# Two attention layers with expert rows: layer 0's latents and the last layer as one program, the last layer's attention opened tile by tile behind the last expert sums

## The chip, the cores and the metric

The kernel runs on one core of one Trainium2 chip. The metric is the device time of one execution in microseconds (us), the median of the runs. Its engines are TensorE (PE; PEld is its weight load), VectorE (DVE), ScalarE (ACT), GpSimd (POOL) and SyncE (SP). SP, ACT and POOL issue DMAs on queues of their own (q1, q10, q0), which are served by the same 16 DMA engines.

## What is computed

A first block (two layers of mLSTM, MoBA and NSA mixers with a feed-forward of 4096) turns `x` [256, 1024] into the latents of a second block of two layers. Only the second block matters here. `c` stands for 256 context rows:

```
def second_block(x, c, ctx, ...):
    for i in range(2):
        h  = rms_norm(x, norm1_gain[i]) * (1 + sc1) + sh1;   hc = the same of xc with the context's rows
        q, k, v    = project_qkv(h, w_qkv[i], ...)    # 8 query heads, 2 key/value heads, 128 wide; rope for x only
        qc, kc, vc = project_qkv(hc, w_qkv[i], ...)
        o = latent_global_attention(...) if i == 0 else latent_window_attention(..., sink)   # 512 keys: 256 of x, 256 of xc
        x = x + g1 * (o @ w_o[i])
        if i == 0: xc = xc + cg1 * (context_attention(...) @ w_o[i])
        h2 = rms_norm(x, norm2_gain[i]) * (1 + sc2) + sh2
        x = x + g2 * peer_ffn(h2, ...)
        if i == 0: xc = xc + cg2 * peer_ffn(h2c, ...)
    return x

def peer_block(hb, w_q, sub_keys, u_tab, v_tab):     # per token: 8 heads x 16 experts out of 16384
    q = (hb @ w_q);  s1, s2 = its halves @ sub_keys;  top 16 of the sums of the top 16s -> expert, g = softmax
    act = gelu(u_tab[expert] . hb);  return sum((g * act) * v_tab[expert])
```

All is float32. So each of the 256 tokens needs 128 expert rows per layer, each a pair of u and v (2 x 1024 numbers, 8 KB).

## The kernel before

`build` (L2464) runs programs one after the other; each is a `Stage` (L101) with a block of instructions per engine, and `Stage.run` (L139) ends it with a barrier of all engines that also clears the semaphores. The order is: context attention; first block with the context's expert rows beside it (`Beside`, L1303); latents (`attention` with part "latents", then `experts` for layer 0, one program); last (`attention` with part "last", `experts` for layer 1, one program); and a last program that stores `x`.

PSUM is four pairs of banks. A stage lists its groups of matmuls in `order`; group number i gets pair i mod 4, one semaphore counts the groups computed, and one per pair counts how often it was emptied. So the list fixes PE's order.

`attention`, part "last" (`h_tiles` 0 to 3: tiles 0 and 1 are `x`, 2 and 3 the context). ACT issues the parameters' loads (L339 to L362): norm gain, context rows, mod rows. SP waits for the first mod rows (L300) and then loads three blocks of w_qkv into the three `ring` buffers, w_o after them (L309). DVE brings the context up to date (L558, L561), ACT squares all four tiles (L377), DVE norms all four (L551, L553), PE turns each (L168) and ACT copies them to `hT` (L383). PE then projects (L174) in the order K/V of tiles 0 and 1, K/V of 2 and 3, queries heads 0 to 3 of both tiles, heads 4 to 7. A block here means one tile by 512 columns, 16 matmul records: eight in all. DVE squares, norms and ropes keys and queries (`squared` L579, `finished` L593, POOL takes the power -0.5 at L762), PE turns them (`QT`), and a loop over 16 heads (tile, head) runs score, window add and maximum (L672, L674), exponential (L436), transposition and value product, with the first tile's output projection among the steps. Then `Early` (L1071) computes the query and scores of head 0, DVE routes it (`route_first` L1114), and POOL issues the first gathers while tile 1's output projection and second norm still run.

`experts` (L1025) has 16 turns (head f, tile g; tile 1 of head 7 last) of 16 rows, 256 in all, in batches of four. POOL gathers row n, one expert pair for each of 128 tokens, into slot n mod ns (`gather`, L1058). It waits until row n - ns is summed. DVE does the dot with `H` (L1148), and per batch the weights (L1151), ACT the tanh and four diagonals (L1218), PE the sums `acc` of v rows (L1267, L1273). ns is 14 for layer 0 and 15 for layer 1, of which 8 are free while the front still runs. SP loads w_q in 1 MB pieces into two halves of ring buffer 2. Queries, scores and routing of the turns ahead run between the batches. At the end DVE adds both tiles' sums to `x` (L1200, L1202), after all 256 rows.

## Time and profile before

| | us |
|---|---|
| median of 3 runs | 3256.99 |
| lowest, highest | 3243.01, 3263.39 |
| profiled execution, its own time | 3264.11 |
| span of its instructions | 3262.3 |
| PE busy in the span | 2631.4 (81%) |
| DVE busy | 1815.7 (56%) |
| POOL busy | 1266.9 (39%) |
| ACT busy | 479.6 (15%) |
| row gathers (q0), share of the 16 DMA engines | 62.2% |
| loads of SP's queue (q1), the same | 18.4% |

The profile is of one execution. A busy share is a mean over stages with different limits; so the slices and windows of the span are read first, and then the timeline of one stretch. In a timeline row the bracket at the end is the engine's idle time ahead of the instruction and what ended it.

### The profile page before, as it was taken

What the parts mean: (1) busy time and instruction counts of PE and PEld (TensorE: products, weight loads), DVE (VectorE), ACT (ScalarE), POOL (GpSimd) and SP (SyncE); (2) the same over time, 40 slices, a digit from 0 to 9 for tenths busy, and PEclk for the clock granted to TensorE, in tenths of its full rate; (3) what the DMA queues carried; (4) which work ended last, traced back from release to release, by engine and by line L of the source; (5) the groups of instructions that cost most, each with busy time, mean ns of one, the idle gap of its engine ahead of it and who ended that gap; (6) DMA issues with size and microseconds to landing.
All of it is one profiled execution on the core that took longest, in us unless ns stands there. A gap on an engine that the chain in (4) does not pass through costs nothing. (4 is left out here: it accounts for less than half of the span.)

```text
span 3262.3 us, 26724 instructions
## 1 busy us (share of the span) xinstructions
PE 2631.4 (81%) x8976; PEld 1410.5 (43%) x8976; DVE 1815.7 (56%) x4659; ACT 479.6 (15%) x1403; POOL 1266.9 (39%) x1072
## 2 busy tenths in 40 slices
PE   6786797999886699966778888888768788888876
PEld 2354555764433377421345343443334544334332
DVE  1438557687113256422148677777526677677774
ACT  0210221000111100000111111111112211111111
POOL 0000535452445367445534444454300254444442
PEclk9898886999997899977899999998978999999999
DMA  6656867797778679899859999999842499999996
GB/s 264 262 212 232 305 227 231 276 366 271 282 294 290 213 293 406 330 346 315 299 193 414 419 419 418 422 421 421 361 172 72 178 415 419 419 418 421 421 421 279
DMA packets 249212, 1046.83 MB, mean 321 GB/s; under 512 B 20550, under 2 KB 53430, under 8 KB 176884
## 3 DMA queue, kind: packets, MB, share of 16 engines
q0 software_dynamic: 147456, 805.37, 62.2%
q1 hardware_dynamic: 93456, 222.23, 18.4%
q10 hardware_dynamic: 8164, 17.53, 1.5%
q8 instruction: 72, 1.18, 0.1%
q14 instruction: 64, 0.52, 0.0%
HBM read 1041.28 MB, written 3.77 MB: 320 GB/s over the span
## 5 line engine op out<-in xcount | busy, mean ns | idle before, releaser
L1456 POOL DMA_INDIRECT sb_beside_slots<-in_peer_uv,sb_beside_chosen x256 | 357.4, 1396 | 394.5 <-DVE sb_beside_slots L1356 207.3
L1356 DVE SCALAR_TENSOR_TENSOR sb_beside_slots<-sb_beside_slots,sb_beside_H 128x1024 f32<-128x1024 f32 x256 | 304.2, 1220 | 120.4 <-DMA sb_beside_slots<-in_peer_uv,sb_beside_chosen 86.8
L1456 POOL DMA_INDIRECT sb_beside_slots<-in_peer_uv,sb_beside_small x256 | 249.8, 976 | 248.1 <-PE psum L1413 172.3
L174 PE MATMUL psum<-sb_f_arena,sb_f_ring 128*128 128x256 f32 (+1 forms) x1344 | 299.8, 386 | 9.3 <-issue 9.3
L174 PEld LDWEIGHTS psum<-sb_f_arena,sb_f_ring 128*128 128x128 f32 (+1 forms) x1344 | 253.4, 189 | 56.6 <-issue 13.9
L1413 PE MATMUL psum<-sb_beside_slots,sb_xc 128*32 128x512 f32 x1024 | 166.8, 783 | 120.3 <-DMA sb_beside_slots<-in_peer_uv,sb_beside_small 98.9
L174 PE MATMUL psum<-sb_f_ring,sb_f_arena 128*128 128x512 f32 (+2 forms) x448 | 191.9, 588 | 2.0 <-ACT sb_f_arena L1773 2.0
L1273 PE MATMUL psum<-sb_beside_slots,sb_latents_scores 128*128 128x512 f32 x304 | 151.2, 650 | 33.4 <-ACT sb_latents_scores L1228 33.3
L2403 PE MATMUL psum<-sb_f_ring,sb_f_arena 128*128 128x512 f32 x384 | 165.4, 592 | 0.0
L1273 PE MATMUL psum<-sb_latents_ring,sb_latents_scores 128*128 128x512 f32 x288 | 137.9, 630 | 26.7 <-ACT sb_latents_scores L1228 26.7
L1273 PE MATMUL psum<-sb_last_ring,sb_last_scores 128*128 128x512 f32 x272 | 129.9, 626 | 24.5 <-ACT sb_last_scores L1228 24.5
L1068 POOL DMA_INDIRECT sb_beside_slots<-in_peer_uv,sb_latents_scores x76 | 88.2, 1160 | 135.8 <-PE psum L1273 91.5
L174 PEld LDWEIGHTS psum<-sb_f_ring,sb_f_arena 128*128 128x128 f32 x448 | 85.8, 194 | 106.6 <-issue 103.8
L1068 POOL DMA_INDIRECT sb_latents_ring<-in_peer_uv,sb_latents_scores x72 | 91.0, 1264 | 92.4 <-PE psum L1273 85.5
L1413 PEld LDWEIGHTS psum<-sb_beside_slots,sb_xc 128*32 128x32 f32 x1024 | 35.1, 130 | 209.3 <-issue 185.9
L1148 DVE SCALAR_TENSOR_TENSOR sb_beside_slots<-sb_beside_slots,sb_latents_H 128x1024 f32<-128x1024 f32 x76 | 92.0, 1224 | 47.7 <-DMA sb_beside_slots<-in_peer_uv,sb_latents_scores 46.4
L1068 POOL DMA_INDIRECT sb_last_ring<-in_peer_uv,sb_last_scores x68 | 82.3, 1210 | 81.7 <-PE psum L1273 74.2
L2403 PEld LDWEIGHTS psum<-sb_f_ring,sb_f_arena 128*128 128x128 f32 x384 | 72.9, 190 | 91.4 <-issue 91.4
L1273 PEld LDWEIGHTS psum<-sb_beside_slots,sb_latents_scores 128*128 128x128 f32 x304 | 62.0, 208 | 115.6 <-issue 73.0
L1148 DVE SCALAR_TENSOR_TENSOR sb_latents_ring<-sb_latents_ring,sb_latents_H 128x1024 f32<-128x1024 f32 x72 | 87.0, 1224 | 42.5 <-DMA sb_latents_ring<-in_peer_uv,sb_latents_scores 42.5
L1148 DVE SCALAR_TENSOR_TENSOR sb_last_ring<-sb_last_ring,sb_last_H 128x1024 f32<-128x1024 f32 x68 | 82.1, 1223 | 34.6 <-DMA sb_last_ring<-in_peer_uv,sb_last_scores 34.6
L1273 PEld LDWEIGHTS psum<-sb_latents_ring,sb_latents_scores 128*128 128x128 f32 x288 | 56.8, 201 | 102.2 <-issue 66.3
(566 smaller groups left out, 4655.3 us busy)
## 6 DMA issues: line engine op xcount, KB each, us to landing
sb_f_ring<-in_w_ff SPq DMA_DIRECT2D x32, 2048.0 KB
sb_context_ring<-in_ada_w SPq DMA_DIRECT2D x23, 2048.0 KB, 13.3
sb_f_ring<-in_w_in SPq DMA_DIRECT2D x8, 2048.0 KB
sb_f_ring<-in_w_in SPq DMA_DIRECT2D x6, 1904.0 KB
sb_context_ring<-in_peer_w_q SPq DMA_DIRECT2D x8, 1024.0 KB, 10.1
sb_f_ring<-in_w_out SPq DMA_DIRECT2D x4, 2048.0 KB
sb_latents_ring<-in_peer_w_q SPq DMA_DIRECT2D x8, 1024.0 KB
sb_last_ring<-in_peer_w_q SPq DMA_DIRECT2D x8, 1024.0 KB, 25.4
```

Of the source, the lines that this page charges most:

```text
L174: last = e.matmul(out, a, b, start=(i == 0), stop=(i == len(terms) - 1))
L1068: e.indirect_dma_start(out=slots[n % ns], out_offset=None, in_=table, in_offset=bass.IndirectOffsetOnAxis(ap=rt["idx"][:, q % 4, k:k + 1], ...
L1148: e.scalar_tensor_tensor(out=u_of(n), in0=u_of(n), scalar=1.0, in1=H[:, turns[n // TOPK][0], :], op0=ALU.mult, op1=ALU.mult, accum_out=rt[ ...
L1273: done = e.matmul(st.pair(("acc", g))[:, half, :], diag[:, n % (4 * BATCH), :], v_of(n)[:, half * 512:(half + 1) * 512], start=(f == 0 and ...
L1356: e.scalar_tensor_tensor(out=row, in0=row, scalar=1.0, in1=self.H[:, t, :], op0=ALU.mult, op1=ALU.mult, accum_out=self.dots[t][:, s:s + 1] ...
L1413: done = e.matmul(self.sums[32 * j:32 * j + 32, half, :], self.columns[:, j, i % 16, :], rows[j][:, half * 512:(half + 1) * 512], start=(i ...
L1456: e.indirect_dma_start(out=self.slots[i % self.SLOTS], out_offset=None, in_=self.table, in_offset=bass.IndirectOffsetOnAxis(ap=at, axis=0) ...
L2403: done = e.matmul(acc[t][:, half, :], u_part[c][:, f * S + t * P:f * S + (t + 1) * P], w[:, f, half * 512:(half + 1) * 512], start=False, ...
```

## The change

The two last attention layers become one program. `last_attention` replaces part "last" of `attention`; it hands out an `Opening`, pieces that the first `experts` calls inside its last turn and behind it: `scalar_first` (square of tile 0), `vector_first_stats`, `vector_first` (norm of tile 0), `gpsimd_first`, `tensor_keys` (turning the sub keys, between the sums of batches 61 and 62), `tensor_first` (transposition and K/V projection of tile 0, behind the last sums), `scalar_first_turned` and `vector_context`. All loads of this attention are issued by SP, each behind a wait for the rows whose slot it overwrites.

The update of `x` is split by tile: tile 0, whose sums end with row 239, is added behind batch 60, tile 1 at the end. In the last layer each tile is stored once it is updated.

PE's order becomes: tile 0's transposition, K/V and first query block; tiles 2 and 3 with their K/V; tile 1 with its K/V; then query blocks one tile at a time. Tile 1's queries are normed and roped in the head loop's steps 1 to 3 and turned in steps 6 and 7.

Memory: layer 0 has 12 row slots instead of 14 (8 of them early, as before), since `gains` and `mod` are wanted earlier; layer 1 has 14 instead of 15, 9 of them early instead of 8. Its w_q pieces go through ring buffer 1.

The diff, cut to its core ("..." marks what is left out):

```diff
@@ def last_attention, new @@
+    order = ["subT", ("hT", 0), ("qkv", 2, 0), ("qkv", 0, 0), ("hT", 2), ("hT", 3), ("qkv", 2, 2), ("hT", 1), ("qkv", 2, 1),
+             ("qkv", 1, 0), ("QT", 0, 0), ("qkv", 0, 1), "KT", ("qkv", 1, 1), ("QT", 1, 0)]
+    tail = lambda g: [("oT", g), ("wo", g, 0), ("wo", g, 1), ("h2T", g)]
+    among = {6: ("QT", 0, 1), 7: ("QT", 1, 1), **dict(zip((9, 10, 12, 16), tail(0)))}
...
+    turns = [2, 3, 0] + [(2, 3, 0, 1)[i % 4] for i in range(len(order) - 3)]
+    st = Stage(nc, sems, psum, order, before.st, turns=turns)
...
+    def sync(e):
+        e.wait_ge(before.sc_copied, 2 * PH)
+        e.wait_ge(before.q_done, 2 * PH)
+        e.wait_ge(*before.landed(before.n_rows - 8))
+        e.dma_start(sub[:, 0:2, :], A["peer_sub_keys_2"][layer].rearrange("a k d -> k a d")).then_inc(sub_in, 16)
+        e.dma_start(gains[:, 0, :], A["norm1_gain_2"][layer:layer + 1, :].to_broadcast([P, D])).then_inc(gains_in[0], 16)
+        for j in (1, 0):
+            e.dma_start(mod[:, j, :], row_of(0, j)).then_inc(mods_in[0], 16)
+        e.dma_start(ring[2], chunk(wqkv, 2)).then_inc(w_in[2], 16)
+        e.wait_ge(before.added, before.n_rows - 8)
+        for j in (1, 0):
+            e.dma_start(modc[:, j, :], row_of(1, j)).then_inc(mods_in[1], 16)
+        for t in range(NT):
+            e.dma_start(work[:, t * D:(t + 1) * D], kept["xc"][:, t, :]).then_inc(xc_in, 16)
+        e.dma_start(work[:, 2 * D:3 * D], kept["mod0"][1:2, 5 * D:6 * D].to_broadcast([P, D])).then_inc(xc_in, 16)
+        e.wait_ge(before.added, before.n_rows - 6)
+        e.dma_start(ring[0], chunk(wqkv, 0)).then_inc(w_in[0], 16)
+        e.wait_ge(before.added, before.n_rows - 4)
+        e.dma_start(ring[1], chunk(wqkv, 1)).then_inc(w_in[1], 16)
+        for j, name in enumerate(("q_norm_gain_2", "k_norm_gain_2")):
+            e.dma_start(qkg[:, j, :], A[name][layer:layer + 1, :].to_broadcast([P, HD2])).then_inc(late_in, 16)
+        e.dma_start(sink[:, :], A["attn_sinks_2"][0:1, :].to_broadcast([P, H2])).then_inc(late_in, 16)
+        e.wait_ge(before.added, before.n_rows)
+        e.dma_start(sb["late"][:, :], A["late"]).then_inc(late_in, 16)
+        e.wait_ge(before.updated, NT)
+        e.dma_start(mod[:, 2, :], row_of(0, 2)).then_inc(gate_in, 16)
+        e.dma_start(gains[:, 1, :], A["norm2_gain_2"][layer:layer + 1, :].to_broadcast([P, D])).then_inc(gains_in[1], 16)
+        e.wait_ge(h_ready, 4)
+        for j in (1, 0):
+            e.dma_start(mod[:, j, :], row_of(0, 3 + j)).then_inc(mods_in[2], 16)
+        e.wait_ge(*st.computed(("qkv", 2, 1)))
+        e.dma_start(ring[wo_ring[0]], chunk(wo, 0)).then_inc(w_in[wo_ring[0]], 16)
+        e.wait_ge(*st.computed(("qkv", 0, 1)))
+        e.dma_start(ring[wo_ring[1]], chunk(wo, 1)).then_inc(w_in[wo_ring[1]], 16)
...
+    def scalar_first(e):
+        e.wait_ge(before.updated, 1)
+        squared_row(e, 0, H[:, 0, :])
+
+    def scalar_first_turned(e):
+        transposed(e, ("hT", 0))
+
+    def scalar(e, early):
+        e.wait_ge(before.added, before.n_rows)
+        kept_rows(e, 2, 0)
+        for g in (2, 3):
+            e.wait_ge(xc_ready, g - 1)
+            squared_row(e, g, work[:, 3 * D:4 * D] if g == 2 else flat(hTc, "p k n -> p (k n)")[:, 0:D])
+        e.wait_ge(before.updated, NT)
+        squared_row(e, 1, H[:, 1, :])
+        kept_rows(e, 0, 0)
+        transposed(e, ("hT", 2))
+        transposed(e, ("hT", 3))
+        transposed(e, ("hT", 1))
+        kept_rows(e, 2, 2)
+        kept_rows(e, 2, 1)
+        kept_rows(e, 1, 0)
...
+    def vector_first_stats(e):
+        deviation(e, rs1[:, 0:1], ss1[:, 0:1], 1)
+
+    def vector_first(e):
+        e.wait_ge(*st.computed("subT"))
+        e.tensor_copy(sub[:, 2:4, :].rearrange("p a n -> p (a n)"), st.pair("subT")[:, 0, 0:2 * P]).then_inc(*st.empties("subT"))
+        scaled(e, mod, 0, mods_in[0], 32)
+        normed(e, 0, rs1[:, 0:1], mod, 1)
+
+    def vector_context(e):
+        e.wait_ge(xc_in, 48)
+        for t in range(NT):
+            e.tensor_tensor(xs[2 + t], xs[2 + t], work[:, 2 * D:3 * D], ALU.mult).then_inc(*own.up())
+        e.wait_ge(*own.now)
+        for t in range(NT):
+            e.tensor_tensor(xs[2 + t], xs[2 + t], work[:, t * D:(t + 1) * D], ALU.add).then_inc(xc_ready, 1)
+        scaled(e, modc, 0, mods_in[1], 32)
+        deviation(e, rs1[:, 1:3], ss1[:, 1:3], 3)
+
+    def vector(e, early):
+        normed(e, 2, rs1[:, 1:2], modc, 2)
+        deviation(e, rs1[:, 3:4], ss1[:, 3:4], 4)
+        normed(e, 3, rs1[:, 2:3], modc, 2)
+        normed(e, 1, rs1[:, 3:4], mod, 3)
...
+        for turn, name in enumerate(((0, 0), "K", (1, 0))):
+            squared(name, work[:, 0:1024])
+            finished(name, 4 + turn, work[:, 1024:2048])
...
+            if i == 1:
+                squared((0, 1), later)
+            if i == 2:
+                finished((0, 1), 7, later)
+                squared((1, 1), later)
+            if i == 3:
+                finished((1, 1), 8, later)
+                scaled(e, mod, 1, mods_in[2], 32)
...
+    def gpsimd_first(e):
+        power(e, 1, rs1, 1)
+
+    def gpsimd(e, early):
+        for turn, (r, n) in enumerate(((rs1[:, 1:3], 2), (rs1[:, 3:4], 1), (rs[:, 0:4], 4), (rs[:, 32:40], 8), (rs[:, 8:12], 4), (rs[:, 4:8], 4), (rs[:, 12:16], 4), (rs2[:, 0:1], 1))):
+            power(e, turn + 2, r, n)
+        early.gather(e)
+        power(e, 10, rs2[:, 1:2], 1)
...
+    def tensor_keys(e):
+        e.wait_ge(sub_in, 16)
+        e.wait_ge(before.q_copied, 2 * PH)
+        ps = st.pair("subT")
+        flip(e, ps[:, 0, 0:P], sub[:, 0, :], ident)
+        flip(e, ps[:, 0, P:2 * P], sub[:, 1, :], ident).then_inc(st.mm, 1)
+
+    def tensor_first(e):
+        e.wait_ge(before.sc_copied, 2 * PH)
+        e.wait_ge(h_ready, 1)
+        transposes(e, ("hT", 0), hn(0))
+        e.wait_ge(before.updated, 1)
+        qkv(e, 2, 0)
+
+    def tensor(e, early):
+        qkv(e, 0, 0)
+        for g in (2, 3):
+            e.wait_ge(h_ready, g)
+            transposes(e, ("hT", g), hn(g))
+        e.wait_ge(before.updated, NT)
+        qkv(e, 2, 2)
+        e.wait_ge(h_ready, 4)
+        transposes(e, ("hT", 1), hn(1))
+        qkv(e, 2, 1)
+        qkv(e, 1, 0)
+
+        def queries_turned(c, g):
+            ps = opened(e, ("QT", c, g))
+            e.wait_ge(y_ready, {(0, 0): 1, (1, 0): 3, (0, 1): 4, (1, 1): 5}[c, g])
+            for j in range(4):
+                done = flip(e, ps[:, 0, j * P:(j + 1) * P], Y[:, g, (4 * c + j) * HD2:(4 * c + j + 1) * HD2], ident)
+            done.then_inc(st.mm, 1)
+
+        queries_turned(0, 0)
+        qkv(e, 0, 1)
+        ps = opened(e, "KT")
+        e.wait_ge(y_ready, 2)
+        for a in range(KV2):
+            for g in range(4):
+                done = flip(e, ps[:, a, g * P:(g + 1) * P], Y[:, g, (H2 + a) * HD2:(H2 + a + 1) * HD2], ident)
+        done.then_inc(st.mm, 1)
+        qkv(e, 1, 1)
+        queries_turned(1, 0)
+        e.wait_ge(*st.emptied("KT"))
+        for c in range(2):
+            e.wait_ge(*st.emptied(("QT", c, 0)))
...
@@ def experts @@
-    st = Stage(nc, sems, psum, [("acc", g) for g in range(NT)], front.st)
+    st = Stage(nc, sems, psum, [("acc", g) for g in range(NT)], front.st, signals=False)
-    wq_half = [sb["ring"][2][:, 2048 * j:2048 * (j + 1)].rearrange("p (k n) -> p k n", k=KT) for j in range(2)]
+    wq_half = [sb["wq_ring"][:, 2048 * j:2048 * (j + 1)].rearrange("p (k n) -> p k n", k=KT) for j in range(2)]
-    prod = u_of(0)
+    prod = sb["gains"][:, 1, :]
...
-        e.nop()
+        if out is not None:
+            tiles = out.rearrange("o (t p) d -> p (o t) d", p=P)
+            for g in range(NT):
+                e.wait_ge(updated, g + 1)
+                e.dma_start(tiles[:, g, :], xs[g]).then_inc(stored, 16)
+            e.wait_ge(stored, 16 * NT)
...
-        if n == ns - 2:
+        if n == n_early + 4:
...
+        if opening:
+            opening.gpsimd_first(e)
...
+        def update(g):
+            e.wait_ge(added, n_rows - (TOPK if g == 0 else 0))
+            e.wait_ge(*own.now)
+            if g:
+                e.wait_ge(updated, g)
+            e.tensor_tensor(prod.rearrange("p (b n) -> p b n", b=2), st.pair(("acc", g))[:, :, :], mod[:, 2, :].rearrange("p (b n) -> p b n", b=2), ALU.mult).then_inc(*own.up())
+            e.wait_ge(*own.now)
+            e.tensor_tensor(xs[g], xs[g], prod, ALU.add).then_inc(updated, 1)
...
+                if b == n_rows // BATCH - 4:
+                    update(0)
+                if opening and b == n_rows // BATCH - 3:
+                    opening.vector_first_stats(e)
+                if opening and b == n_rows // BATCH - 2:
+                    opening.vector_first(e)
             if ahead(q):
                 keep_scores(ahead(q))
-        for g in range(NT):
-            if g == 0:
-                e.wait_ge(added, n_rows)
-            e.wait_ge(*own.now)
-            e.tensor_tensor(prod.rearrange("p (b n) -> p b n", b=2), st.pair(("acc", g))[:, :, :], mod[:, 2, :].rearrange("p (b n) -> p b n", b=2), ALU.mult).then_inc(*own.up())
-            e.wait_ge(*own.now)
-            e.tensor_tensor(xs[g], xs[g], prod, ALU.add).then_inc(*own.up())
-
-    def scalar(e):
+        if opening:
+            opening.vector_context(e)
+        update(1)
...
+            if opening and q == len(turns) - 1:
+                opening.scalar_first(e)
...
             if ahead(q):
                 scores(ahead(q))
+            if opening and q == len(turns) - 1:
+                opening.tensor_keys(e)
             sums(4 * q + 2)
             sums(4 * q + 3)
-
-    st.run(sync, scalar, vector, gpsimd, tensor, beside and beside.sems[0])
+        if opening:
+            opening.tensor_first(e)
...
@@ def layer_memory, def last_memory (new) @@
-    slots = [*spare]
-    if last:
-        at = 3584 + ROUTE_COLS
-        slots += [mod[:, 3:5, :].rearrange("p k n -> p (k n)"), pair(H, 1)]
-        slots += [big[:, at + 2048 * j:at + 2048 * (j + 1)] for j in range(2)]
-    slots += [work[:, 0:2048], work[:, 2048:4096], aux[:, 0:2048]]
-    sb["n_early"] = len(slots)
-    slots += [ring[:, j // 2, 2048 * (j % 2):2048 * (j % 2 + 1)] for j in range(4)]
-    slots += [flat(sb["hT2"][:, :, :], "p k n -> p (k n)")[:, 2048:4096]] if last else []
-    slots += [pair(gains, 0), pair(mod, 0)]
-    sb["slots"] = slots
+    halves = lambda j: [ring[:, j, 0:2048], ring[:, j, 2048:4096]]
+    flat_pair = lambda a, j: flat(a[:, 2 * j:2 * j + 2, :], "p k n -> p (k n)")
+    early = [flat_pair(spare, j) for j in range(3)] + [aux[:, 0:2048], flat_pair(spare, 3), flat(beside_H[:, :, :], "p t n -> p (t n)"), work[:, 0:2048], work[:, 2048:4096]]
+    sb["slots"], sb["n_early"], sb["wq_ring"] = early + halves(0) + halves(1), len(early), sb["ring"][2]
+    return sb
+
+
+def last_memory(sb, spare, beside_H, xc):
+
+
+    sb = dict(sb)
+    early = [flat(xc[:, :, :], "p t n -> p (t n)")] + sb["slots"][0:sb["n_early"]]
+    sb["Y"] = flat(spare[:, 0:6, :], "p k n -> p (k n)").rearrange("p (g n) -> p g n", g=4)
+    sb["hTc"] = flat(spare[:, 6:8, :], "p k n -> p (k n)").rearrange("p (k n) -> p k n", k=KT)
+    sb["modc"] = beside_H
+    sb["QT2"] = sb["big"][:, 0:5120].rearrange("p (h n) -> p h n", h=10)
+    halves = lambda r: [r[:, 0:2048], r[:, 2048:4096]]
+    sb["slots"] = early + halves(sb["ring"][2]) + halves(sb["ring"][0]) + [flat(sb["mod"][:, 0:2, :], "p k n -> p (k n)")]
+    sb["n_early"], sb["wq_ring"] = len(early), sb["ring"][1]
...
@@ def build @@
+                former = experts(nc, sems, psum, sb, A, C, xs, 0, front, beside)
+                front, opening = last_attention(nc, sems, psum, sb_last, A, C, xs, kept, former)
+                latter = experts(nc, sems, psum, sb_last, A, C, xs, 1, front, out=out)
...
+                def sync(e):
+                    former.sync(e)
+                    latter.sync(e)
...
+                latter.st.run(sync, scalar, vector, gpsimd, tensor, beside.sems[0])
```

## Rows read from the trace of the kernel before

**Rows 1.** The page, part 2: GB/s moved in 40 slices of 81.56 us.

```profile
GB/s 264 262 212 232 305 227 231 276 366 271 282 294 290 213 293 406 330 346 315 299 193 414 419 419 418 422 421 421 361 172 72 178 415 419 419 418 421 421 421 279
```

**Rows 2.** Windows from:to, width, busy us (instructions) per engine, TensorE clock, DMA share, GB/s.

```profile
2200.00:2300.00 100.00, 83.16 (x168) 34.31 (x167) 71.26 (x199) 17.51 (x64) 47.82 (x42) 0.90 1.01 421
...
2360.00:2380.00 20.00, 12.03 (x24) 4.69 (x22) 7.86 (x11) 1.69 (x6) 0.00 (x0) 0.84 0.01 4
...
2420.00:2440.00 20.00, 20.00 (x48) 8.79 (x47) 0.00 (x0) 1.02 (x1) 0.00 (x0) 1.00 0.00 1
...
2500.00:2520.00 20.00, 17.93 (x108) 12.48 (x107) 16.34 (x46) 9.25 (x26) 0.00 (x0) 1.00 0.00 1
```

**Rows 3.** Timeline (start us, us, engine, line, operation, idle before and releaser), POOL.

```profile
2571.99 1.01 POOL L1068 DMA_INDIRECT sb_xc<-in_peer_uv,sb_last_scores  x1 [22.57 <-DVE sb_last_scores L1139]
```

**Rows 4.** Timeline, DVE: the dots of row 248 and of row 255.

```profile
2345.96 1.22 DVE L1148 SCALAR_TENSOR_TENSOR sb_latents_ring<-sb_latents_ring,sb_latents_H 128x1024 f32<-128x1024 f32 x1 [0.32 <-DMA sb_latents_ring<-in_peer_uv,sb_latents_scores]
...
2363.29 1.23 DVE L1148 SCALAR_TENSOR_TENSOR sb_beside_slots<-sb_beside_slots,sb_latents_H 128x1024 f32<-128x1024 f32 x1 [1.23 <-DMA sb_beside_slots<-in_peer_uv,sb_latents_scores]
```

**Rows 5.** Timeline, PE; the line without an engine's form is of the chain of waits.

```profile
2365.95 8.83 PE L1273 MATMUL psum<-sb_beside_slots,sb_latents_scores 128*128 128x512 f32 x16 [2.76 <-ACT sb_latents_scores L1228]
...
2413.98 57.11 PE L174 MATMUL psum<-sb_last_ring,sb_last_hT 128*128 128x512 f32 x128 [1.43 <-ACT sb_last_hT L383]
...
2413.98 43.39 PE psum L174 x96
...
2487.60 3.75 PE L880 MATMUL psum<-sb_last_scores 128*128 128x512 f32 x4 [0.88 <-ACT sb_last_scores L417]
...
2556.72 3.48 PE L174 MATMUL psum<-sb_last_hT,sb_last_ring 128*128 128x128 f32 x29 [0.27 <-issue]
```

**Rows 6.** Timeline, ACT's first load of layer 1 and the scale row.

```profile
2381.09 0.30 ACTq L339 DMA_DIRECT2D sb_last_crow<-in_c  x1
...
2396.94 2.36 DVE L538 SCALAR_TENSOR_TENSOR sb_last_mod<-sb_last_mod,sb_last_gains 128x1024 f32<-128x1024 f32 x2 [0.84 <-DMA sb_last_mod<-kept_mod]
```

**Rows 7.** Timeline, one mod row and its taker; tile ring of layer 1, loads, issue to landing.

```profile
2578.01 0.33 ACTq L468 DMA_DIRECT2D sb_last_mod<-kept_mod  x1
...
2586.53 1.22 DVE L1148 SCALAR_TENSOR_TENSOR sb_xc<-sb_xc,sb_last_H 128x1024 f32<-128x1024 f32 x1 [1.57 <-DMA sb_last_mod<-kept_mod]
...
DMA to landing us min/median/max: 8.3/25.1/32.8
```

**Rows 8.** Timeline, DVE: a rope instruction, and the first operation of three heads.

```profile
2480.55 0.42 DVE L612 TENSOR_TENSOR sb_last_work<-sb_last_scores,sb_last_aux 128x256 f32<-128x256 f32 x1
...
2489.68 0.69 DVE L672 TENSOR_TENSOR sb_last_work<-psum,sb_last_aux 128x512 f32<-128x512 f32 x1 [3.85 <-PE psum L880]
...
2500.67 0.68 DVE L672 TENSOR_TENSOR sb_last_work<-psum,sb_last_aux 128x512 f32<-128x512 f32 x1
...
2505.95 0.69 DVE L672 TENSOR_TENSOR sb_last_work<-psum,sb_last_aux 128x512 f32<-128x512 f32 x1 [0.18 <-PE psum L880]
```

**Rows 9.** Timeline, POOL and DVE: first gather of layer 0, dot of row 7.

```profile
1693.12 0.99 POOL L1068 DMA_INDIRECT sb_beside_slots<-in_peer_uv,sb_latents_scores  x1 [24.08 <-DVE sb_latents_scores L1139]
...
1719.69 1.23 DVE L1148 SCALAR_TENSOR_TENSOR sb_latents_aux<-sb_latents_aux,sb_latents_H 128x1024 f32<-128x1024 f32 x1 [1.26 <-DMA sb_latents_aux<-in_peer_uv,sb_latents_scores]
```

**Rows 10.** Timeline, POOL: gather of row 119; DVE: dot of row 117.

```profile
1998.99 1.04 POOL L1068 DMA_INDIRECT sb_latents_aux<-in_peer_uv,sb_latents_scores  x1 [1.94 <-PE psum L1273]
...
2011.63 1.23 DVE L1148 SCALAR_TENSOR_TENSOR sb_latents_work<-sb_latents_work,sb_latents_H 128x1024 f32<-128x1024 f32 x1 [0.38 <-DMA sb_latents_work<-in_peer_uv,sb_latents_scores]
```

**Rows 11.** Timeline, POOL and DVE: gather and dot of row 30.

```profile
1773.52 1.32 POOL L1068 DMA_INDIRECT sb_beside_slots<-in_peer_uv,sb_latents_scores  x1 [3.19 <-PE psum L1273]
...
1784.08 1.23 DVE L1148 SCALAR_TENSOR_TENSOR sb_beside_slots<-sb_beside_slots,sb_latents_H 128x1024 f32<-128x1024 f32 x1 [0.72 <-DMA sb_beside_slots<-in_peer_uv,sb_latents_scores]
```

**Rows 12.** Timeline, the end: last dot, last update instruction, store.

```profile
3241.50 1.23 DVE L1148 SCALAR_TENSOR_TENSOR sb_xc<-sb_xc,sb_last_H 128x1024 f32<-128x1024 f32 x1 [1.25 <-DMA sb_xc<-in_peer_uv,sb_last_scores]
...
3255.16 1.22 DVE L1202 TENSOR_TENSOR sb_x<-sb_x,sb_xc 128x1024 f32<-128x1024 f32 x1
...
3257.52 0.38 SPq L2510 DMA_DIRECT2D out<-sb_x  x1
```

423 lines of the change are left out of this document (332 added, 91 removed).

## Prediction

> **What bounds the kernel now.** Read the slices of the page first. The row of GB/s is the one to follow: in slices 22 to 28 it stands near 420, falls to 172, 72 and 178 for three slices of 81.6 us, and comes back to 415 to 422 until near the end [rows 1]. The two plateaus are the expert stages of the two attention layers. The windows say the same at closer range: 421 GB/s at a DMA share of 1.01 with PE busy 83 of 100 us in the first plateau, then 4 and 1 GB/s between the two [rows 2]. In the plateaus the DMA engines are the bound: each row gather moves 128 x 8 KB = 1.05 MB, and the last eight dots start 2.48 us apart (17.33 us for seven steps), each after a wait for its gather [rows 4].
>
> POOL issues the first gather of layer 1 at 2571.99 [rows 3]; the last dot of layer 0 starts at 2363.29 [rows 4]. For 208.7 us no gather runs. The last stage then needs 3241.50 - 2571.99 = 669.5 us from its first gather to its last dot, the one before needed 2363.29 - 1693.12 = 670.2 [rows 3, 4, 9, 12]. So what pulls the gather at 2571.99 forward pulls the end forward by as much, unless a plateau becomes slower. I follow the chain through this gap.
>
> **The gap in pieces.** Row 248, the first of the last eight, starts its dot at 2345.96 [rows 4]; I call this A. The last sums run on PE from 2365.95 to 2374.78, A+28.8; I call their end T [rows 5]. Then come the update of x, the barrier, loads issued from 2381.09 on, a scale row that waits for one of them until 2396.94 [rows 6], four norms and transposes, eight blocks of projection from 2413.98 on (57.1 us), norms and turning of the queries, and the first scores at 2487.60, T+112.8 [rows 5]. The heads last to 2556.72, 69.1 us. The early query, the routing of one head and the first gather take 15.3 us more.
>
> **What is taken out and added up to the heads.** The barrier goes, and the loads' wait in series, and the norm of all four tiles ahead of any projection. Norm, transposition and K/V projection of tile 0 go around the last expert sums. Before T this costs:
> - The update of tile 0 (two DVE instructions of 1.22 us [rows 12], 2.5) moves ahead of the dots of batch 61. DVE is free for 1.23 us in front of a dot [rows 4], so two rows take it up: nothing.
> - At A, SP issues the sub keys (0.13 MB), a gain and two mod rows (1.6 MB) and 2 MB of w_qkv. DVE waits for the first four in `vector_first`. Behind this wait stand the four dots of batch 63, their weights, ACT's diagonals and PE's last sums; nothing fills it. How long is it? Alone, loads pass quickly: the shortest weight load (1 MB) lands after 8.3 us. But seven gathers are in flight, and beside gathers the longest took 32.8. One mod row of the same size, issued at 2578.01 into running gathers, lets DVE go at 2586.53, 8.5 us [rows 7]. I take 8.5 for the first such row, 4 for each of the two behind it in the same queue, 5.5 for the small one: A+22. Bounds: A+11 (hardly held up; then the last gather's landing sets the dots) and A+31 (8.5 for each).
> - From A+22: scale row 1.2, norm 2.5, four dots without a wait 4.6, weights and diagonals 1.4 (2364.52 to 2365.95), sums 8.8 [rows 4 to 6] gives the new end of the sums, T' = A+40.5. T was A+28.8: 11.7 us later (bounds 4 and 21).
>
> The Trainium skill (DMA: Bandwidth & Descriptors, Queues, rings and completion order) says that each DMA engine goes round its queues packet by packet. If one load and one row gather took turns, a mod row would cost 1.25 + 2.5 = 3.75 us and three 11.3. By this estimate the sum would be some 5 us better; the 8.5 us row bears on it and is slower.
>
> After T' the PE order is: transposes, K/V and first queries of tile 0, transposes and K/V of tiles 2 and 3, the same of tile 1, then three query blocks with the turning of queries and keys between them. PE sets this stretch:
> - Eight blocks, as many as now. Six with their slow start take 43.39, the last two 57.11 - 43.39 = 13.7, so 6.87 each [rows 5]: 55.0.
> - Flips: four transposes of 1.1, turning 0.5, 1.0 and 0.6 (eight flips take 1.04 to 1.1): 6.5.
> - Waits, from laying the engines side by side: ACT's copy of hT 1.6. DVE's norms of tiles 2 and 3, 2.0 and 1.5; they start only when the update of tile 1 is through at T'+15.8, since DVE first waits for ACT's squares of the context, which stand behind K/V of tile 0 (T'+12.9). Copies of 1.4, 1.4 and 1.0. Sum 8.9.
>
> Together 70.4 against 112.8: 42.4 less. The barrier itself is small in it (four updates end at 2379.8, ACT issues at 2381.09). K's DVE work and the POOL powers lie beside projections; if that cover went, K's 10 us would stand in PE's way. The rest of q1's traffic, 8 MB with two more w_qkv blocks and the context rows, is through near A+46, ahead of each use; the late constants, issued at T', are wanted at T'+27.
>
> **The heads.** DVE now norms and turns the second tile's queries inside head steps 1 to 3. For each of two blocks: a square and a reduce of 0.69 (512 columns), 0.17, two multiplications of 0.69, six rope instructions 0.34 apart [rows 8], 5.0. With the scale row, 1.2, that now runs ahead of the loop: 11.3. Two heads take 5.28 us (2500.67 to 2505.95 [rows 8]) with DVE busy 16.3 and PE 17.9 of 20 us [rows 2]: little room. But before the first head's scores DVE waits 3.85 us [rows 8], and the first three heads run slower than the rest; I take 3.4 of this as gone. 69.1 + 11.3 - 3.4 = 77.0, 7.9 more (bounds 0 and 12). The tail as now, 15.3.
>
> First gather: 11.7 - 42.4 + 7.9 = 22.8 us earlier.
>
> **The slots.** The first plateau gets 12 row slots instead of 14, the second 14 instead of 15. The second change costs nothing: with 14 and 15 slots the plateaus took 670.2 and 669.5. For 12, ask what a gather needs when nothing is queued: issued at 1693.12; the eighth dot waits until 1719.69; less seven rows of 2.48, 9.2 us [rows 9]. With two slots fewer a gather is issued when today the one two places on is. In steady running the tightest place leaves 2011.63 - 1998.99 = 12.6 us, over 9.2 [rows 10]. In the start-up a row issued at 1773.52 has its dot at 1784.08 with 14 slots [rows 11]: no queue is left, and two slots fewer lose 1 to 4 us in each of one or two places. I take 4 (0 to 10).
>
> The same page (Anatomy of one DMA) gives 2 us plus bytes over 436 GB/s, here 4.4 us. By that the slots would cost nothing; no row here shows so short a gather.
>
> **The end.** Of four update instructions two run ahead, the store is half as large and follows without a barrier (3256.38 to 3257.52 now [rows 12]): 2.5 + 1.1 + 0.6 = 4.2 (3 to 6).
>
> **Sum.** -22.8 + 4 - 4.2 = -23.0. The profiled execution took 3264.1 (span 3262.3), so 3241; against the median of 3257.0, 7 lower, 3234.
>
> **Rivals.**
> - *Short waits:* the loads land by A+11 and the head steps hide DVE's extra work. For it, DVE's 3.85 us ahead of the heads; against it, 16.3 of 20 us busy after. -23 - 7.7 - 7.9 = -39: 3218.
> - *The loads hold DVE longer,* 8.5 us each. For it, the 32.8. T' is 9 later: 3243.
> - *Slower: 12 slots starve the first plateau.* A slot's round trip is now 14 x 2.48 = 34.7 us. If that were latency and not queueing, 12 slots would give a row every 2.89 us: 256 rows, 105 more, 3335. It takes the whole gain (27 us without the 4) from a round trip of 31.0 on (0.105 us a row), and is 1% slower from 32.6. Against: the rows above met 2.48 with 10.6 and 12.6 us in hand [rows 10, 11].
> - *No change in effect:* T' 21 later, heads 12 longer, slots 10: 21 - 42.4 + 12 + 10 - 4.2 = -4: 3253.
>
> **How the numbers follow.** The forecast case (3226 to 3241) has 0.57, short waits 0.18, longer loads 0.13, no effect 0.07, starved 0.05. The range holds all but the starved case and the outer ends of two others: 3214 to 3253. About 1% (32.6 us) is what a measurement can tell, so 3224.4 and 3289.6 are the bounds. Faster needs most of the short waits, or slots that cost nothing beside part of them: 0.20. Slower is the starved case: 0.05. The rest, 0.75, is within 1%.
>
> **What would show it.** Right: the first gather of layer 1 comes some 19 us sooner; before the last four dots DVE waits about 10 us for mod rows, and then they run back to back; PE idles under 10 us between T' and the heads; the head loop is some 8 us longer; both plateaus at 418 to 421 GB/s. Wrong: a first plateau under 415 GB/s, a wait for mod rows under 4 or over 20 us, PE gaps ahead of the heads, or a head loop of 69 us.

## The result, and the profile of the kernel after

The changed kernel takes 3239.3 us (median of 20 runs, 3233.8 to 3246.1), the kernel before 3258.6 (20 runs, 3243.0 to 3266.3). The ratio is 0.9944, interval [0.9936, 0.9952]: 19.3 us less, 0.6%. The forecast was 23 us less. The profiled execution of after has a span of 3237.4 us, that of before 3262.3.

The page of after, its slices of DMA share and GB/s (40 equal slices of 80.9 us):

```profile
DMA  6656866797778679989859999999952599999996
GB/s 266 263 190 243 294 239 217 276 385 278 279 267 314 240 273 406 360 325 319 305 180 391 419 419 419 420 421 417 421 192 78 204 407 418 419 418 421 421 421 288
```

Beside [rows 1], the two plateaus stand at the same height, the hole between them is filled a little (192, 78, 204 for 172, 72, 178), and the first plateau starts lower: the 100 us that begin 10 us after its first gather have 395 GB/s, in before 414. From 20 us after the first gather on, 620 us of the first plateau have 416 GB/s (before: 419).

The two gathers at the hole's rims, on POOL, timeline of after (start, duration, engine, line, operation, in brackets the idle time before it and who ended it):

```profile
2339.47 0.95 POOL L1501 DMA_INDIRECT sb_second_aux<-in_peer_uv,sb_second_scores  x1 [0.30 <-issue]
2547.59 1.01 POOL L1501 DMA_INDIRECT sb_xc<-in_peer_uv,sb_second_scores  x1 [22.05 <-DVE sb_second_scores L1583]
```

The first gather of layer 1 is issued at 2547.59, against 2571.99 in [rows 3]: 24.4 us sooner. Of these, 7.0 are no work of the change: the first gather of layer 0 came at 1686.17 in this execution and at 1693.12 in that of before [rows 9], and everything up to there is unchanged. 17.4 us are left.

The place where DVE waits for the mod rows, timeline of DVE in after (the short accumulator reads left out):

```profile
2342.10 1.23 DVE L1592 SCALAR_TENSOR_TENSOR sb_second_ring<-sb_second_ring,sb_second_H 128x1024 f32<-128x1024 f32 x1 [0.24 <-DMA sb_second_ring<-in_peer_uv,sb_second_scores]
...
2362.58 1.23 DVE L1082 SCALAR_TENSOR_TENSOR sb_second_mod<-sb_second_mod,sb_second_gains 128x1024 f32<-128x1024 f32 x1 [10.02 <-DMA sb_second_mod<-kept_mod]
2363.92 1.28 DVE L1091 SCALAR_TENSOR_TENSOR sb_second_H<-sb_x,sb_second_small,sb_second_mod 128x1024 f32<-128x1024 f32 x1
2365.24 1.23 DVE L1093 TENSOR_TENSOR sb_second_H<-sb_second_H,sb_second_mod 128x1024 f32<-128x1024 f32 x1
2366.38 1.22 DVE L1592 SCALAR_TENSOR_TENSOR sb_beside_slots<-sb_beside_slots,sb_second_H 128x1024 f32<-128x1024 f32 x1
2367.52 1.22 DVE L1592 SCALAR_TENSOR_TENSOR sb_beside_slots<-sb_beside_slots,sb_second_H 128x1024 f32<-128x1024 f32 x1
```

A is 2342.10, the dot of row 248. The mod rows let DVE go at A+20.5 after 10.02 us of idle time; scale row, norm, and then the four dots 1.15 us apart, as forecast.

PE from the last sums to the heads, timeline of PE in after:

```profile
2372.48 7.40 PE L1723 MATMUL psum<-sb_beside_slots,sb_second_scores 128*128 128x512 f32 x12 [12.80 <-ACT sb_second_scores L1674]
2379.72 1.88 PE L1723 MATMUL psum<-sb_second_aux,sb_second_scores 128*128 128x512 f32 x4
2381.43 1.04 PE L171 MATMUL psum<-sb_consts,sb_second_H 128*128 128x128 f32 x8
2383.68 13.97 PE L177 MATMUL psum<-sb_second_ring,sb_second_hT 128*128 128x512 f32 x32 [1.21 <-ACT sb_second_hT L1001]
2398.68 1.09 PE L171 MATMUL psum<-sb_consts,sb_xc 128*128 128x128 f32 x8 [1.03 <-DVE sb_xc L1093]
2401.20 1.09 PE L171 MATMUL psum<-sb_consts,sb_xc 128*128 128x128 f32 x8 [1.43 <-DVE sb_xc L1093]
2403.50 15.67 PE L177 MATMUL psum<-sb_second_ring,sb_beside_slots 128*128 128x512 f32 x32 [1.21 <-ACT sb_beside_slots L1001]
...
2451.60 1.96 PE L1342 MATMUL psum<-sb_second_scores 128*128 128x512 f32 x4 [0.94 <-ACT sb_second_scores L1035]
2455.33 0.63 PE L171 MATMUL psum<-sb_consts,sb_second_work 128*128 128x128 f32 x4 [1.78 <-ACT sb_second_work L1056]
...
2468.31 0.76 PE L171 MATMUL psum<-sb_consts,sb_second_work 128*128 128x128 f32 x4 [4.92 <-ACT sb_second_work L1056]
...
2475.66 1.09 PE L171 MATMUL psum<-sb_consts,sb_second_work 128*128 128x128 f32 x4 [3.31 <-ACT sb_second_work L1056]
```

The last sums end at 2381.6 (A+39.5) and the first scores start at 2451.60: 70.0 us, where [rows 5] had 112.8. In the head loop PE stands still for 4.92 and 3.31 us; in both places it waits for ACT's exponentials, and these for DVE's maxima, which stand behind tile 1's query work in DVE's order. DVE itself stood idle ahead of the loop, before its first instruction:

```profile
2452.73 0.69 DVE L1196 TENSOR_TENSOR sb_second_work<-psum,sb_second_aux 128x512 f32<-128x512 f32 x1 [7.21 <-PE psum L1342]
```

The end, timeline of after:

```profile
3219.11 1.23 DVE L1592 SCALAR_TENSOR_TENSOR sb_beside_slots<-sb_beside_slots,sb_second_H 128x1024 f32<-128x1024 f32 x1 [1.24 <-DMA sb_beside_slots<-in_peer_uv,sb_second_scores]
...
3230.64 1.22 DVE L1554 TENSOR_TENSOR sb_second_gains<-psum,sb_second_mod 128x1024 f32<-128x1024 f32 x1 [9.36 <-PE psum L1723]
3231.90 1.22 DVE L1556 TENSOR_TENSOR sb_x<-sb_x,sb_second_gains 128x1024 f32<-128x1024 f32 x1
3233.15 0.36 SPq L1488 DMA_DIRECT2D out<-sb_x  x1
```

Two update instructions instead of four, and the store right behind them; the last dot is 18.3 us before the end, 20.8 in before [rows 12].

### The profile page after: what moved, and what is told of

The parts are those of the page before. It is cut to its first block, busy times and chain, and to the rows that moved or that the text cites. A ratio compares the mean times of both kernels' runs of the same rounds, so it can differ in the third digit from the quotient of the medians.

```text
span 3237.4 us, 26712 instructions
## 1 busy us (share of the span) xinstructions
PE 2627.7 (81%) x8974; PEld 1406.6 (43%) x8974; DVE 1817.8 (56%) x4670; ACT 479.7 (15%) x1406; POOL 1257.0 (39%) x1076
## 3 DMA queue, kind: packets, MB, share of 16 engines
HBM read 1041.27 MB, written 3.77 MB: 323 GB/s over the span
## 4 chain that ended last, share of the span: by engine, by line
DMA 23%; PE 21%; DVE 7%; POOL 3%; issue 2%; ACT 1%; SPq 0%; DVEq 0%; another core or an unknown queue 0%; ACTq 0%; POOLq 0%
PE psum L1723 11%; PE psum L177 7%; DMA sb_beside_slots<-in_peer_uv,sb_second_scores 5%; DMA sb_second_ring<-in_peer_uv,sb_second_scores 5%; DMA sb_second_work<-in_peer_uv,sb_second_scores 3%; DMA sb_second_aux<-in_peer_uv,sb_second_scores 3%; DMA sb_beside_slots<-in_peer_uv,sb_beside_small 2%; PE psum L1867 2%; DMA sb_second_ring<-in_peer_w_q 2%; POOL sb_beside_slots L1910 1%; DMA sb_second_mod<-in_peer_uv,sb_second_scores 1%; DMA sb_second_mod<-kept_mod 1%; POOL sb_beside_slots L1501 1%; DVE sb_second_scores L1430 1%; DVE sb_second_scores L1433 1%
## 5 line engine op out<-in xcount | busy, mean ns | idle before, releaser
L1723 PE MATMUL psum<-sb_beside_slots,sb_second_scores 128*128 128x512 f32 x648 | 334.7, 662 | 97.1 <-ACT sb_second_scores L1674 95.6
L1723 PE MATMUL psum<-sb_second_ring,sb_second_scores 128*128 128x512 f32 x624 | 302.1, 636 | 60.5 <-ACT sb_second_scores L1674 60.5
L1501 POOL DMA_INDIRECT sb_beside_slots<-in_peer_uv,sb_second_scores x162 | 199.1, 1229 | 282.8 <-PE psum L1723 222.0
L1501 POOL DMA_INDIRECT sb_second_ring<-in_peer_uv,sb_second_scores x156 | 196.7, 1261 | 200.2 <-PE psum L1723 184.4
L1723 PEld LDWEIGHTS psum<-sb_beside_slots,sb_second_scores 128*128 128x128 f32 x648 | 134.0, 212 | 275.6 <-issue 155.7
L1592 DVE SCALAR_TENSOR_TENSOR sb_second_ring<-sb_second_ring,sb_second_H 128x1024 f32<-128x1024 f32 x156 | 188.5, 1223 | 91.2 <-DMA sb_second_ring<-in_peer_uv,sb_second_scores 90.9
L1592 DVE SCALAR_TENSOR_TENSOR sb_beside_slots<-sb_beside_slots,sb_second_H 128x1024 f32<-128x1024 f32 x162 | 195.9, 1222 | 76.0 <-DMA sb_beside_slots<-in_peer_uv,sb_second_scores 75.0
L1674 ACT ACTIVATE sb_second_scores<-sb_consts,sb_second_scores 128x128 f32<-128x128 f32 x512 | 163.8, 391 | 38.5 <-DVE sb_second_scores L1604 34.9
L1723 PE MATMUL psum<-sb_second_work,sb_second_scores 128*128 128x512 f32 x312 | 148.3, 615 | 13.0 <-ACT sb_second_scores L1674 13.0
L177 PE MATMUL psum<-sb_second_ring,sb_second_hT 128*128 128x512 f32 x320 | 141.3, 598 | 3.7 <-ACT sb_second_hT L1001 1.9
```

What stands on the lines that cost most here:

```text
L177: last = e.matmul(out, a, b, start=(i == 0), stop=(i == len(terms) - 1))
L1501: e.indirect_dma_start(out=slots[n % ns], out_offset=None, in_=table, in_offset=bass.IndirectOffsetOnAxis(ap=rt["idx"][:, q % 4, k:k + 1], ...
L1592: e.scalar_tensor_tensor(out=u_of(n), in0=u_of(n), scalar=1.0, in1=H[:, turns[n // TOPK][0], :], op0=ALU.mult, op1=ALU.mult, accum_out=rt[ ...
L1674: e.activation(diag[:, (b % 4) * BATCH + r, :], C("ident"), ACT.Copy, scale=w[:, r:r + 1]).then_inc(diag_ready, 1)
L1723: done = e.matmul(st.pair(("acc", g))[:, half, :], diag[:, n % (4 * BATCH), :], v_of(n)[:, half * 512:(half + 1) * 512], start=(f == 0 and ...
```

## The experiments

Each experiment was profiled, so it can be read by its stages as well as by its time. The stages matter here: over the 14 profiled executions the first gather of layer 0 came anywhere from 1685.5 to 1697.2 us, though all of them do the same work up to there. The table gives, for each profile: from the first gather of layer 0 to A; from A to the start of the last dot; from A to the end of the last sums (T); from T to the first scores; from there to the first gather of layer 1; the sum, first gather to first gather; from there to the last dot; from it to the end. All were worked out from starts and durations in the timelines of POOL, DVE and PE. The last column is the median time. Eight kernels are the same up to A (after, norm_late, loads_late, loads_series, kv_after_norms, heads_moved, no_tile1_work, combo); their first stage takes 654.8 to 657.0 us, so some 2 us in one row of this column are scatter. The medians come from four comparisons in which before itself stood at 3258.6, 3259.7, 3261.2 and 3261.8 us; kernels of different comparisons are set side by side by their ratios to before.

| kernel | gather to A | last dot | T | to scores | to gather | gather to gather | to last dot | to end | median |
|---|---|---|---|---|---|---|---|---|---|
| before | 652.8 | A+17.3 | A+28.8 | 112.8 | 84.4 | 878.9 | 669.5 | 20.8 | 3258.6 |
| before_again | 653.0 | A+17.4 | A+27.2 | 111.0 | 82.8 | 874.0 | 669.5 | 22.5 | 3258.9 (one run) |
| slots_only | 655.2 | A+17.3 | A+27.2 | 109.8 | 82.8 | 874.9 | 670.5 | 22.5 | 3264.6 |
| after | 655.9 | A+27.7 | A+39.5 | 70.0 | 96.0 | 861.4 | 671.5 | 18.3 | 3239.3 |
| rows_early | 660.4 | A+21.5 | A+33.7 | 70.8 | 95.8 | 860.7 | 670.7 | 16.5 | 3241.2 |
| all_early | 665.4 | A+19.0 | A+31.3 | 70.8 | 95.8 | 863.3 | 670.8 | 16.6 | 3242.3 |
| norm_late | 657.0 | A+22.0 | A+34.6 | 71.0 | 95.9 | 858.5 | 671.5 | 18.3 | 3239.9 |
| loads_late | 654.8 | A+17.8 | A+30.5 | 71.2 | 95.9 | 852.4 | 670.8 | 16.6 | 3231.3 |
| loads_series | 655.8 | A+17.8 | A+29.3 | 85.3 | 95.7 | 866.0 | 671.0 | 16.6 | 3243.9 |
| kv_after_norms | 655.3 | A+27.7 | A+39.9 | 80.0 | 96.2 | 871.4 | 670.6 | 16.6 | 3249.4 |
| heads_moved | 655.7 | A+27.7 | A+40.2 | 70.9 | 88.2 | 854.9 | 671.8 | 16.5 | 3236.5 |
| no_tile1_work | 655.3 | A+27.8 | A+40.0 | 70.8 | 84.2 | 850.3 | 670.7 | 18.1 | 3234.3 |
| combo | 655.9 | A+17.8 | A+27.6 | 73.9 | 88.2 | 845.6 | 670.6 | 18.2 | 3226.5 |
| combo_rows | 659.8 | A+17.3 | A+27.2 | 69.9 | 88.2 | 845.0 | 671.8 | 16.5 | 3228.7 |

The theory on trial is the sum of the prediction: loads that hold DVE ahead of the last sums, a shorter way from there to the heads, DVE's extra work in the heads, a few us for the slots. The rivals are that the wait has another nature, that the heads hide the work, and that the slots cost nothing or much.

**The wait for the mod rows: three ways to be rid of it.** The first, rows_early, issues the same rows sooner:

```
-        e.wait_ge(*before.landed(before.n_rows - 8))
+        e.wait_ge(*before.landed(before.n_rows - 24))
         e.dma_start(sub[:, 0:2, :], ...)
         ...                                    # gain, two mod rows
+        e.wait_ge(*before.landed(before.n_rows - 8))
         e.dma_start(ring[2], chunk(wqkv, 2))
```

> Kernel after, but the sub keys, the gain and the two mod rows of tile 0 are issued 16 rows (about 40 us) sooner; w_qkv stays where it was. Theory (the loads' wait stands on the path of the last sums): DVE's idle 10.0 us before the scale row goes, while 1.7 MB pass among the gathers instead, at 419 GB/s 4.1 us that row 248 comes later. Net 6 us less than after: about 3233 us. Rival A (bandwidth is not tight enough to matter): the full 10 us, 3229. Rival B (the end of the last sums does not set what follows, because the w_qkv block or the squares do): the wait goes but K/V of tile 0 starts no sooner, 3239 or a few us more.

Measured: 3241.2 us, ratio to before 0.9945 [0.9929, 0.996], where after has 0.9944. My 3233 was wrong, and rival B's number (3239 or a few more) came true, but not its cause: K/V of tile 0 does start sooner, at A+35.8 for A+41.6. The price was right: first gather to A is 4.5 us longer, for 1.7 MB. But the last dot comes only 6.2 us sooner, not 10: with the rows there, two of the last four dots wait for their gathers by 1.17 and 2.02 us. What was gained at the last sums (5.8) was mostly paid in the plateau (4.5).

The second, all_early, is the first hunk without the second, so w_qkv goes early too:

> As rows_early, but the first w_qkv block (2.1 MB) goes with the rows 16 rows sooner. Theory (in the plateau every byte costs its time at 419 GB/s): row 248 comes 5.0 us later than in rows_early, and nothing waits less for it, so 5 us more than rows_early, 3238. Rival A (room is left beside the gathers): the same as rows_early. Rival B (the w_qkv block held K/V of tile 0 back): less than rows_early.

Measured: 3242.3 us, 0.9955 [0.9939, 0.9971]. First gather to A grows by another 5.0 us for another 2.1 MB, exactly the bandwidth's price. But the last sums come 2.4 us sooner (A+31.3 for A+33.7), since this block no longer passes beside the last gathers; I had expected no such return. Gather to gather is 2.6 over rows_early, not 5; the two medians can't be told apart.

The third, norm_late, leaves the loads and moves the waiting instruction:

```
-                if opening and b == n_rows // BATCH - 2:
-                    opening.vector_first(e)
         ...
         if opening:
+            opening.vector_first(e)
             opening.vector_context(e)
```

> Kernel after, but the scale row and the norm of tile 0 stand behind the dots and weights of the last batch instead of ahead of them. Theory (the placement itself made the last sums wait for the mod rows): the last dots wait only for their gathers, the last sums end at A+29 instead of A+39.5 (A: start of the dot of row 248), DVE has the scale row at about A+21.7 and the norm at A+24.2, still ahead of the end of the sums, so the transposes of tile 0 start up to 10 us sooner: 3230 us, range 3228 to 3234. Rival (the norm is then late for PE, by scale row, norm and the copies, some 5 us or more in series after the sums, and the loads are late as well): 3237 to 3243.

Measured: 3239.9 us, 0.9935 [0.9922, 0.9949]; I had expected 3230. The rival's range, 3237 to 3243, holds it, and half of its cause is there: the loads are late, but the norm is not, since the transposes follow the last sums without a pause. By its time it can't be told from after; by stages it is 2.9 us better, gather to gather (4.1 from A on), and the reason why it is not 9 stands in its last four dots, timeline of DVE in norm_late:

```profile
2361.43 1.23 DVE L1592 SCALAR_TENSOR_TENSOR sb_beside_slots<-sb_beside_slots,sb_second_H 128x1024 f32<-128x1024 f32 x1 [1.05 <-DMA sb_beside_slots<-in_peer_uv,sb_second_scores]
...
2365.20 1.22 DVE L1592 SCALAR_TENSOR_TENSOR sb_beside_slots<-sb_beside_slots,sb_second_H 128x1024 f32<-128x1024 f32 x1 [2.53 <-DMA sb_beside_slots<-in_peer_uv,sb_second_scores]
...
2368.97 1.23 DVE L1592 SCALAR_TENSOR_TENSOR sb_beside_slots<-sb_beside_slots,sb_second_H 128x1024 f32<-128x1024 f32 x1 [2.53 <-DMA sb_beside_slots<-in_peer_uv,sb_second_scores]
...
2372.45 1.23 DVE L1592 SCALAR_TENSOR_TENSOR sb_second_aux<-sb_second_aux,sb_second_H 128x1024 f32<-128x1024 f32 x1 [2.25 <-DMA sb_second_aux<-in_peer_uv,sb_second_scores]
```

Nothing of DVE's own stands between them, and yet they are 3.77, 3.77 and 3.48 us apart instead of 2.48. The loads slow the gathers themselves. So the 10.02 us in after were not only a wait of one instruction behind its loads: behind it stood gathers that were late as well, hidden by it. The Trainium skill (DMA: Bandwidth & Descriptors, Queues, rings and completion order) says that a DMA engine goes round its queues packet by packet, so a queue of loads takes turns with the queue of gathers; the spacing, 3.77 us for 2.48, agrees in kind.

**The loads behind the last gather.** If loads and gathers share, the loads should start when the gathers are through. On top of norm_late:

```
         e.dma_start(sub[:, 0:2, :], ...)
+        e.wait_ge(*before.landed(before.n_rows - 1))
         e.dma_start(gains[:, 0, :], ...)
```

> As norm_late, and the gain, the mod rows and the first w_qkv block are issued only once the last row gather has landed (the sub keys stay where they were). In norm_late the last four dots were 3.5 to 3.8 us apart instead of 2.48 and the last sums ended at A+34.6. Theory (the wait is not one of order but of bytes: loads and the last gathers share the DMA engines): with nothing beside them the last dots are 2.48 apart again, last dot A+17.3, last sums A+28.8; gain and rows then land alone, some 6 to 9 us after A+17, norm at A+27 to A+30, w_qkv before A+34. First scores about A+100 to A+103 against 105.5 in norm_late and 109.5 in after: 3233 to 3237 us. Rival (a fixed cost of each load, not the sharing, spaced the dots): last dot at A+22 again and the loads later still, so 3 us or more slower than norm_late, 3243.

Measured: 3231.3 us, 0.9915 [0.99, 0.9929], a little under the 3233 to 3237 expected; the first scores come at A+101.7, as expected. Gather to gather is 9.0 us under after; 1.1 of these lie ahead of A, where the two kernels are the same, so 7.9 are the placement's, and 3.8 of them come on top of norm_late. The last dots, timeline of DVE in loads_late, are 2.46 to 2.48 us apart again, and then DVE waits for the mod rows with no dot behind it:

```profile
2356.62 1.23 DVE L1593 SCALAR_TENSOR_TENSOR sb_beside_slots<-sb_beside_slots,sb_second_H 128x1024 f32<-128x1024 f32 x1 [1.24 <-DMA sb_beside_slots<-in_peer_uv,sb_second_scores]
...
2359.08 1.23 DVE L1593 SCALAR_TENSOR_TENSOR sb_second_aux<-sb_second_aux,sb_second_H 128x1024 f32<-128x1024 f32 x1 [1.23 <-DMA sb_second_aux<-in_peer_uv,sb_second_scores]
...
2367.61 1.23 DVE L1083 SCALAR_TENSOR_TENSOR sb_second_mod<-sb_second_mod,sb_second_gains 128x1024 f32<-128x1024 f32 x1 [6.02 <-DMA sb_second_mod<-kept_mod]
```

The rows, issued from 2359.07 on, are there at 2367.61, 8.5 us later, and the norm ends at 2371.5, just as the last sums end at 2371.8. That settles the nature of the wait: the same bytes, started some 17 us later, cost 3.8 us less than in norm_late, which differs in nothing else, because they no longer stand in the way of the gathers that the last sums need. The rival with a fixed cost of each load (last dot at A+22 again) is out.

**How much the overlapped loads and the early K/V are worth.** Two undoings. In loads_series the wait of loads_late is on the last expert sum instead (`e.wait_ge(before.added, before.n_rows)`), so that the loads come in series behind the sums, without a barrier:

> As loads_late, but the gain, rows and w_qkv blocks are issued only when the last expert sum is added, so that they come in series as in before; no barrier, tile order kept. Theory (loads in series cost their whole landing, the barrier itself little): issue at A+29, rows land 9 us later, norm and transposes 5 more; K/V of tile 0 starts at A+44 instead of A+33, first scores 10 to 12 us later than in loads_late (A+101.7), 3242 us. Rival (the barrier was what cost, so that loads in series are nearly as good): within 4 us of loads_late.

Measured: 3243.9 us, 0.9937 [0.9919, 0.9955]. First scores at A+114.6 against A+101.7, 12.9 us later, a little over the 10 to 12 expected. (The ratios of the times, 0.9937 and 0.9915, are 7 us apart, and with four and five runs their intervals overlap; the size is read from the stages.) DVE waits 17.39 us for the mod rows and PE 12.44 us for the norm. And this kernel, with its loads as late as before's but no barrier and tile order, still takes 85.3 us from the last sums to the first scores, where before takes 110 to 113. In kv_after_norms PE waits for all four norms ahead of K/V of tile 0, and ACT squares the context first:

```
         e.wait_ge(before.updated, 1)
+        e.wait_ge(h_ready, 4)
         qkv(e, 2, 0)
```

> Kernel after, but the K/V projection of tile 0 waits until all four norms are through (ACT squares the context ahead of keeping it), as in before; program, loads and slots as in after. Theory (42.4 us between the last sums and the first scores come partly from tile 0 being projected while the others are normed): the four norms end about 13 us after the last sums instead of K/V starting at 2.3 us after them, two to four us of waits further on go: first scores 7 to 9 us later than in after, at T+77 to T+79 (after: T+70.0), 3247 us. Rival (the projections wait later anyway for loads or copies, so the early start gains nothing): T+70 to T+72, 3240.

Measured: 3249.4 us, 0.996 [0.9947, 0.9974]; 80.0 us to the scores instead of 70.0, one more than the top of my range. The row, timeline of PE in kv_after_norms:

```profile
2401.55 16.48 PE L177 MATMUL psum<-sb_second_ring,sb_second_hT 128*128 128x512 f32 x32 [13.28 <-DVE sb_second_H L1093]
```

In after PE has 14 us of projections to do while ACT squares and DVE norms the context and tile 1; here it stood idle for 13.28. And 2.5 of the 10.0 us are the clock: these 32 matmuls took 16.48 us at a granted clock of 0.85, and 13.97 at 1.00 in after. So by stages more than half of the change's gain is this one placement. By the ratios of the times it is less, 5 us, and the intervals overlap a little.

**The heads.** First, how much of the loop's growth is DVE's work on tile 1: no_tile1_work leaves out its queries' norm, gain and rope, with two instructions of four columns in place of each block, and puts the second norm's scale row in step 9:

```
             if i == 1:
-                squared((0, 1), later)
+                skipped((0, 1), 7)
             ...
```

> Kernel after without the norm, gain and rope of tile 1's queries (left out: their squares, reduces, scales and rotations, two instructions of four columns stand in for each block), and the scale row in step 9. Theory (DVE's extra work of 11.3 us lies on the path whole): first scores to first gather falls from 96.0 to 84.4, the value of before; 3228 us. Rival (part of the loop's growth is PE's, from its clock or from the turning of tile 1's queries): 88 or more stays.

Measured: 84.2 us from the first scores to the first gather; before has 84.4, and 82.8 in two other profiles. The growth, 11.8 us, is DVE's 11.3 and next to nothing else; no part of it was hidden. (Against 82.8 the growth is 13.2, and 1.4 of it have no shown cause.) Its time is 3234.3 us, 0.9912 [0.9897, 0.9927]: not the 3228 expected, but by the ratios 10 us under after.

heads_moved keeps the work and places it better:

```
         for turn, name in enumerate(((0, 0), "K", (1, 0))):
             ...
+        squared((0, 1), H[:, 1, :])
+        finished((0, 1), 7, H[:, 1, :])
         ...
-            if i == 1:
-                squared((0, 1), later)
             if i == 2:
-                finished((0, 1), 7, later)
                 squared((1, 1), later)
-            if i == 3:
+            if i == 4:
                 finished((1, 1), 8, later)
+            if i == 9:
                 scaled(e, mod, 1, mods_in[2], 32)
```

> Kernel after, but the first query block of tile 1 is squared and normed ahead of the head loop, where DVE waited 7.2 us, the second is squared in step 2 and finished in step 4, and the scale row goes from step 3 to step 9. Theory (DVE's 11.3 us of extra work in steps 1 to 3 lie on the path whole): 5.0 us go into the wait ahead of the loop and 6.3 are spread over steps that have about 0.4 us free each, so first scores to first gather of layer 1 falls from 96.0 to 89 to 91; 3233 to 3235 us. Rival A (the loop is held by PE's half-clock stretches): 96 stays, 3239. Rival B (DVE is full in all steps, so that a spread saves nothing and only the 5.0 of the wait count): 91.

Measured: 88.2 us in the stage, 7.8 less, a little better than either version expected; 3236.5 us, 0.9925 [0.9912, 0.9939], by the ratios 6 us under after (expected 3233 to 3235). Timeline of DVE in heads_moved, the last instruction ahead of the loop and the first one in it:

```profile
2452.30 0.42 DVE L1164 TENSOR_TENSOR sb_beside_slots<-sb_second_H 128x256 f32<-128x256 f32 x1
2453.38 0.69 DVE L1198 TENSOR_TENSOR sb_second_work<-psum,sb_second_aux 128x512 f32<-128x512 f32 x1 [0.66 <-PE psum L1342]
```

The idle time ahead of the first head was 7.21 us in after and is 0.66 here. The first block fits into it whole; of the remaining 6.3 us, moved to steps with a little room, some 2.8 vanish too. The rival that PE's clock holds the loop is out.

**The slots.** The kernel before with 12 slots in the first expert stage and 14 in the second, otherwise as it was:

```
-        if n == ns - 2:
+        if n == n_early + 4:
         ...
-    slots += [flat(sb["hT2"][...])[:, 2048:4096]] if last else []
-    slots += [pair(gains, 0), pair(mod, 0)]
+    slots += [pair(gains, 0)] if last else []
+    slots += [pair(mod, 0)] if last else []
```

> Kernel before with 12 row slots in the first expert stage and 14 in the last, nothing else changed. Theory (the start-up of the first plateau loses by the two slots, the rest does not): first gather to dot of row 248 3.1 us longer than in before (as it is in after), last plateau within 1 us: 3 us more than before. Rival A (the slots cost nothing and the 3.1 us of after have another cause): same as before. Rival B (the last plateau loses too, 2 us, as in after): 5 us more.

Measured: 3264.6 us, 1.0015 [1.0006, 1.0024], 4.9 us over the 3259.7 of before in the same comparison. By stages 2.4 (or 2.2, against before_again) are in the first plateau and 1.0 in the second. The loss is in the first 100 us, as forecast: the dot of row 24 comes 79.9 us after the first gather (before: 79.7), that of row 32 at 103.2 (99.4), that of row 60 at 175.1 (172.6), and from there on 2.4 us stay. Window view of 1700 to 1800 us in slots_only (busy time of each engine with its instructions, granted clock, DMA share, GB/s), where before has 413 and after 396 GB/s:

```profile
1700.00:1800.00 100.00, 76.47 (x238) 44.67 (x239) 73.90 (x214) 18.20 (x63) 45.02 (x38) 0.91 0.99 397
```

The interval reaches from 2 to 8 us, so the theory's 3 and rival B's 5 are not told apart by the times; "no cost" is out, and starvation is out by far. For the first plateau the eight kernels that are the same up to A bear it out: 654.8 to 657.0 us, where before has 652.8 and 653.0. By the sum of the Trainium skill for a DMA (DMA: Bandwidth & Descriptors, Anatomy of one DMA: 4.4 us for a gather by its figures, an estimate), the slots would have cost nothing; these stages show that they cost 2 to 4 us.

**Both improvements together.** combo is loads_late and heads_moved in one, with the scale row in step 10:

> loads_late and heads_moved together, the scale row for the second norm one step later still (step 10, where DVE waited 6.7 us). Theory (both lie in series on the one path): first gather to first gather of the two stages 861.4 - 9.0 - 7.8 - 1.2 = 843 us, 3222 us, 1.1% under before. Rival (what the first gives the second loses, in the clock or in waits for copies): 850, 3229.

Measured: 3226.5 us, 0.9896 [0.988, 0.9911]: 1.0% under before and 13 us under after, the interval clear of after's. Gather to gather takes 845.6 us, the theory said 843 and the rival 850; the time stands midway between their 3222 and 3229. Of the 2 us over the theory's, 1.2 are the scale row, whose other step brought nothing (88.2 again), and 1.1 lie ahead of A (655.9 for 654.8 in loads_late), where nothing differs. So the two improvements add up, and the rival's loss isn't there: from A to the first scores it takes 101.5 us, and 101.7 in loads_late, though by another way. Timeline of PE, twelve of the last sixteen sums in loads_late, and then in combo with what follows them:

```profile
2361.75 8.38 PE L1723 MATMUL psum<-sb_beside_slots,sb_second_scores 128*128 128x512 f32 x12 [2.85 <-ACT sb_second_scores L1674]
```

```profile
2363.26 5.42 PE L1723 MATMUL psum<-sb_beside_slots,sb_second_scores 128*128 128x512 f32 x12 [1.51 <-ACT sb_second_scores L1674]
...
2373.17 1.94 PE L171 MATMUL psum<-sb_consts,sb_second_H 128*128 128x128 f32 x8 [2.78 <-DVE sb_second_H L1094]
2376.31 8.88 PE L177 MATMUL psum<-sb_second_ring,sb_second_hT 128*128 128x512 f32 x16 [1.21 <-ACT sb_second_hT L1002]
```

The last dot stands at A+17.8 in both kernels, but the sixteen last sums took 7.13 us here, at a granted clock of 1.00, and 10.09 in loads_late, at 0.70. They ended sooner (A+27.6), so PE waited 2.78 us for the norm, and then its eight flips took 1.94 us instead of 1.04 and sixteen matmuls 8.88 instead of some 7. The time to the scores is 73.9 us instead of 71.2.

combo_rows issues the rows early again and only w_qkv behind the last gather:

> combo, but gain and rows of tile 0 16 rows sooner as in rows_early, and only the first w_qkv block behind the last gather. Theory: the first plateau is 4.1 us longer for their 1.7 MB, the norm waits for nothing, T comes 1 to 2 us sooner and the 3.85 us that PE waited for the second w_qkv block in loads_late go: 1 to 2 us under combo. Rival (the plateau pays in full and PE is held by something else next): 2 to 4 us over combo.

Measured: 3228.7 us, 0.99 [0.9886, 0.9915], not to be told from combo by its time; by stages 845.0 against 845.6. It pays 3.9 us in the plateau and gets 4.5 back (sums end at A+27.2, 69.9 to the scores). PE's wait for the second w_qkv block is 0.75 us, in combo 1.19. The expected 1 to 2 us under combo are not there by the times.

**A second look at before.** The kernel before, unchanged, once more:

> The kernel before, unchanged, for a second profiled execution to read the terms from. Theory (the sum was made against an execution whose end was short and whose gap was ordinary): from the last dot to the end 22 us as in slots_only, not 20.8, which makes the end term of the change -4 instead of -2.5; from the dot of row 248 to the first gather of layer 1 224 to 227 us. Rival (the gap of 226.0 in the first execution was a long one, and slots_only's 219.7 is the ordinary): 218 to 221, and 20.8 again at the end.

Measured: each side was right in one half. The end is 22.5 us, not 20.8 (theory), and from A to the first gather of layer 1 it takes 221.0 us, not 226.0 (rival); slots_only, the same there, has 219.8. Against them, the execution that the prediction was made against was 5 us long in the gap and 1.7 short at the end. Of the 5 us, 1.7 are the last sums (8.83 us for 7.13) and 1.9 the projections (57.11 for 55.17).

## Why the prediction was right, and where its terms were off

It forecast 3234 us, 3214 to 3253, and most likely within 1% of before; the kernel takes 3239.3, 0.6% under before. The mechanism holds. Term by term, with the first profile of before, and in brackets against its second:

- **Last sums later, +11.7:** 10.7 (12.3). The mod rows let DVE go at A+20.5, forecast A+22. The size was right, but the account of it was too simple, so its fit is in part luck: I had the dots of the last batch wait for loads alone. norm_late shows that the gathers behind them were slowed as well, so that removing DVE's wait alone brings only 4.9 us of it; loads_late shows that keeping the loads out of the gathers' way brings 9.0 in all. Of the bracket's 12.3, some 2 are the clock of the sixteen last sums, 9.12 us in after and 7.13 in the second profile; the forecast took 8.8 for them.
- **From the last sums to the first scores, -42.4:** -42.8 (-41.0). The step that carries the gain was the most exact. Expected waits of 1.6, 2.0, 1.5, 1.4, 1.4 and 1.0 us; the rows of PE show 1.21, 1.03, 1.43, 1.21, 1.16 and 0.94. kv_after_norms puts 10.0 of it on the K/V projection placed ahead of the other norms, and loads_series 12.9 (counted from A, against loads_late) on loads that no longer follow the sums.
- **The heads, +7.9:** +11.6 (+13.2). This is the step that failed. The 11.3 us of DVE's work were right, the 3.4 taken off them were not: I gave back the wait of 3.85 us that DVE has ahead of the first head [rows 8], though the work was placed behind that wait, in steps 1 to 3. In after the wait had even grown, to 7.21 us, with the work standing after it. Only heads_moved puts work there, and then it is free. no_tile1_work shows the full 11.8.
- **The slots, +4:** +3.1 (+2.9), and +2.4 in slots_only. Right, and sized a little high.
- **The second plateau, 0:** +2.0 in after; the ten other kernels of its family have 670.6 to 671.8 against 669.5, so 1.1 to 2.3. Two things are in it. Up to the dot of row 243, slots_only loses 1.0 us for 14 slots in place of 15, and the family 0 to 1.1. And from the dot of row 243 to that of row 255 it is 29.75 us in the three kernels that update and store both tiles at the end, and 30.93 to 30.97 in all eleven others: 1.2 us. The prediction had no term for this one, the store of tile 0, which now runs among the gathers. Timelines of SP and DVE in after:

```profile
3192.79 0.36 SPq L1488 DMA_DIRECT2D out<-sb_x  x1
...
3195.61 1.23 DVE L1592 SCALAR_TENSOR_TENSOR sb_second_work<-sb_second_work,sb_second_H 128x1024 f32<-128x1024 f32 x1 [0.57 <-DMA sb_second_work<-in_peer_uv,sb_second_scores]
3198.85 1.22 DVE L1592 SCALAR_TENSOR_TENSOR sb_second_ring<-sb_second_ring,sb_second_H 128x1024 f32<-128x1024 f32 x1 [2.00 <-DMA sb_second_ring<-in_peer_uv,sb_second_scores]
```

  The dots caught up with the two update instructions by row 246, as the prediction said; the gather of row 247 is the late one. Layer 0 has the same early update and no store, and there the dots of rows 243 and 248 are 13.3 to 13.4 us apart with it and without it (15.3 in all_early, where w_qkv passes too). The store's 0.52 MB at 421 GB/s are 1.25 us. No run left out the store alone.
- **The end, -4.2:** -2.5 against the first profile, -4.2 against the second, and -4.2 to -6.0 in the family (16.5 to 18.3 against 22.5). The term was right; the execution it was measured against was not typical.

The sum of the stages is -18.0 against the first profile (1569.2 to 1551.2 us from the first gather to the end) and -14.7 against the second; the medians say -19.3. The errors of the terms (-1.0, -0.4, +3.7, -0.9, +2.0, +1.7) cancel only in small part: +7.4 in heads, second plateau and end, -2.3 in the other three. The rest is the scatter of single executions, first of all of the start of the stage, and no run assigns it further. Of the signs named, the head loop grew by 11.6 us and not by some 8, and the first plateau has 416 GB/s, under the 418 forecast and over the 415 that would have spoken for starvation.

Of the rivals, short waits was wrong in both parts: the rows came at A+20.5, not A+11, and the heads hid nothing. Loads at 8.5 us each, no effect, and starvation did not come either; longer loads came nearest by its number, 3243, but not by its cause. What pulled the time from 3234 towards it was the heads first (3.7 us), then the second plateau (2.0), and for the heads the error was the share of the short-waits rival that I had let into the sum.

## What to carry over

A wait ahead of a loop is only worth something to work that is placed ahead of the loop: before taking idle time off a sum, check on which side of it the instruction stands. Where transfers of two queues meet at a bound, the wait that shows is that of the instruction first in line, and the transfers that the next ones need are late behind it; price the bytes together, and ask which of them could start after the others. And take the base of a sum from two executions where the sum is a few us: here one was 5 us long in one stage and 1.7 short in another.

## What the runs showed of the hardware

**The last gathers are finished by a small part of the DMA engines.** Windows of 4 us at the end of the first plateau in before (columns as above: the last three are granted clock, DMA share and GB/s):

```profile
2348.00:2352.00 4.00, 4.00 (x9) 1.79 (x8) 2.30 (x3) 0.00 (x0) 0.00 (x0) 0.80 0.97 403
2352.00:2356.00 4.00, 2.97 (x7) 0.95 (x5) 2.02 (x8) 0.81 (x4) 0.00 (x0) 1.00 0.30 125
2356.00:2360.00 4.00, 3.94 (x9) 1.82 (x10) 2.33 (x4) 0.88 (x4) 0.00 (x0) 1.00 0.06 27
2360.00:2364.00 4.00, 3.19 (x8) 1.14 (x6) 1.94 (x3) 0.00 (x0) 0.00 (x0) 1.00 0.04 18
```

and in loads_late, where between the small sub keys (2341.36) and 2359.07 no load was issued:

```profile
2352.00:2356.00 4.00, 4.00 (x10) 1.76 (x10) 2.13 (x4) 0.58 (x2) 0.00 (x0) 1.00 0.06 27
2356.00:2360.00 4.00, 2.89 (x7) 0.95 (x5) 2.15 (x3) 0.00 (x0) 0.00 (x0) 1.00 0.04 16
```

The last dots start 2.48 us apart up to 2363.29 in before [rows 4] and each waits for its gather, but from 2352 on the share falls to 0.30 and then to 0.06 and 0.04, which is about one engine of sixteen (0.0625) or less. At 27 GB/s the 2.48 us of a row move 67 KB, and a sixteenth of a gather is 66. So the gathers that those dots wait for are complete but for a small rest, and the DMA engines that the plateau's mean share of 1.01 shows as evenly full do not finish together: the last ones need some 10 us more. That it is one engine with a sixteenth of each gather fits these numbers, but it is an inference; which engine, and why, no run here tells. It does say that the plateau's pace of 2.48 us a row need not be that of the mean engine.

**The same code is paced by the granted clock of its execution.** The 128 projection matmuls of before took 57.11 us in one execution [rows 5] and 55.17 in the other; window view of that stretch in before, and in before_again:

```profile
2413.00:2471.00 58.00, 57.02 (x129) 25.24 (x130) 14.83 (x28) 3.68 (x4) 4.18 (x2) 0.96 0.32 112
```

```profile
2410.00:2466.00 56.00, 55.43 (x132) 24.80 (x133) 15.14 (x29) 3.50 (x5) 4.19 (x2) 1.00 0.31 114
```

0.96 against 1.00 of the full clock over the stretch, and 1.9 us between them. The sixteen last sums took 7.13 us at 1.00 (combo), 8.83 at 0.81 (before) and 10.09 at 0.70 (loads_late), so T moves by up to 3 us between executions of the same code. In combo the slow first matmuls came after 2.78 us in which PE stood idle; in after and in loads_late PE went from the sums to the flips without a pause, and the flips took 1.04 us, the first sixteen matmuls 7.11 in loads_late.
